# Sparse mixer: index stage reordered, with GpSimd taking part of it, and a search for the largest keys with a wait for each part

## The reference, cut to what matters

```python
def sparse_attention(h, cos, sin, w_in, q_norm, k_norm, w_out, topk):   # topk = 64, two query blocks of 128
    q, k, v, qi, ki, wi = split_cols(h @ w_in, SA_SPLITS)   # 16 heads of q, one k and v, 8 index heads qi, one ki, 8 weights wi
    q = apply_rope(rms_norm(q.reshape(b, L, ATT_HEADS, ATT_HEAD_DIM), q_norm), cos, sin)
    k = apply_rope(rms_norm(k, k_norm)[:, :, None, :], cos, sin)[:, :, 0]
    qi = apply_rope(qi...); ki = apply_rope(ki...)
    logits = einsum('bthd,bsd->btsh', qib, ki)
    score = einsum('btsh,bth->bts', relu(logits), wib) * idx_scale
    score = where(causal, score, -inf)
    _, sel = lax.top_k(score, topk)                          # the 64 keys with the largest score
    ...                                                      # softmax of q.k over the chosen keys, times v, then @ w_out
```

## Time and profile before

| what | value |
|---|---|
| median of 3 runs | 2318.72 us (2318.62 to 2319.46) |
| the profiled execution | 2319.0 us, its span 2317.1 us |
| TensorE busy | 2307.1 us (100%) |
| VectorE busy | 1682.3 us (73%) |
| ScalarE busy | 1256.1 us (54%) |
| GpSimd busy | 79.0 us (3%) |
| stretch of the sparse mixer | about 770 to 872 us from the span's start |

### The profile page before, as it was taken

One profiled execution on the slowest core, in us unless ns is written; L12 is line 12 of the kernel. 1 busy time (PEld: TensorE's weight loads), 2 busy tenths in 40 slices (PEclk: granted clock), 3 DMA queues, 4 the chain that ended last, 5 costly groups with the idle time before them and its releaser, 6 DMA issues.

```text
span 2317.1 us, 32714 instructions
## 1 busy us (share of the span) xinstructions
PE 2307.1 (100%) x13658; PEld 2019.2 (87%) x13658; DVE 1682.3 (73%) x2141; ACT 1256.1 (54%) x1523; POOL 79.0 (3%) x116
## 2 busy tenths in 40 slices
PE   9999999999999999999999999999999999999999
PEld 8889889888888978888888878888888888788887
DVE  8867846876876789768766777587687677776873
ACT  6545664554554565545555764455455467554552
POOL 2000000000000020100010000001000100000000
PEclk9999999999999999999999999999999999999999
DMA  7655435555555525655655534566556555344554
GB/s 228 195 186 178 136 138 195 186 185 186 193 191 183 169 75 189 217 188 189 197 185 181 182 128 146 167 196 210 188 189 194 183 184 169 127 149 161 197 183 145
DMA packets 335042, 409.51 MB, mean 177 GB/s; under 512 B 7894, under 2 KB 285104, under 8 KB 334896
## 3 DMA queue, kind: packets, MB, share of 16 engines
q1 hardware_dynamic: 331632, 401.66, 52.6%
q0 software_dynamic: 3072, 5.69, 0.9%
q10 hardware_dynamic: 192, 0.08, 0.0%
HBM read 406.35 MB, written 1.05 MB: 176 GB/s over the span
## 4 chain that ended last, share of the span: by engine, by line
PE 93%; DVE 4%; DMA 1%; ACT 1%; issue 0%; SPq 0%; DVEq 0%; ACTq 0%
PE bank L614 13%; PE acc L614 12%; PE bank L1384 11%; PE bank L622 7%; PE acc L622 6%; PE acc L706 6%; PE bank L706 6%; PE acc L693 4%; PE bank L713 3%; PE acc L713 3%; PE acc L790 3%; PE acc L2772 2%; PE acc L1554 2%; DVE part_lo L504 1%; PE bank L3349 1%; PE bank L652 1%
## 5 line engine op out<-in xcount | busy, mean ns | idle before, releaser
L504 DVE TENSOR_TENSOR part_lo<-raw,part_hi 128x2048 fp32r<-128x2048 f32 (+3 forms) x390 | 870.4, 2235 | 342.2 <-ACT part_hi L497 338.8
L497 ACT ACTIVATE part_hi<-raw 128x2048 fp32r<-128x2048 f32 (+3 forms) x390 | 728.3, 1868 | 331.6 <-DMA raw<-in_ffn_w 98.9
L614 PE MATMUL bank<-hT,part_hi 128*128 128x512 f32 x1408 | 328.2, 390 | 0.0
L614 PEld LDWEIGHTS bank<-hT,part_hi 128*128 128x128 f32 x1408 | 261.6, 188 | 52.9 <-ACT part_hi L497 0.2
L614 PE MATMUL acc<-hT,part_hi 128*128 128x512 f32 x1280 | 298.2, 390 | 0.0
L614 PEld LDWEIGHTS acc<-hT,part_hi 128*128 128x128 f32 x1280 | 237.7, 188 | 47.7
L1384 PE MATMUL bank<-part_hi,hT 128*128 128x512 f32 x768 | 247.4, 395 | 0.0
L622 PE MATMUL bank<-hT,part_lo 128*128 128x256 f32 x1408 | 184.2, 284 | 0.0
L622 PEld LDWEIGHTS bank<-hT,part_lo 128*128 128x128 f32 x1408 | 178.1, 192 | 3.6
L1384 PEld LDWEIGHTS bank<-part_hi,hT 128*128 128x128 f32 x768 | 144.2, 188 | 31.2 <-issue 1.7
L622 PE MATMUL acc<-hT,part_lo 128*128 128x256 f32 x1280 | 166.4, 283 | 0.2 <-DVE part_lo L504 0.2
(11 more groups left out here) (547 smaller groups left out, 3274.3 us busy)
## 6 DMA issues: line engine op xcount, KB each, us to landing
raw<-in_ffn_w SPq DMA_DIRECT2D x122, 1024.0 KB, 5.2
raw<-in_w_in SPq DMA_DIRECT2D x48, 1024.0 KB, 4.9
raw<-in_ffn_w_up SPq DMA_DIRECT2D x44, 1024.0 KB, 5.2
raw<-in_ffn_w_gate SPq DMA_DIRECT2D x43, 1024.0 KB, 5.2
raw<-in_ffn_w_down SPq DMA_DIRECT2D x32, 1024.0 KB, 5.2
raw<-in_hy_w_in SPq DMA_DIRECT2D x22, 1024.0 KB, 4.9
raw<-in_ffn_w_down SPq DMA_DIRECT2D x16, 768.0 KB, 4.4
raw<-in_ffn_w SPq DMA_DIRECT2D x12, 768.0 KB, 4.5
```

What stands on the lines that cost most here:

```text
L497: t.e.activation(part_hi[:, n % SLOTS, 0:size], raw[:, n % SLOTS, 0:size], ACT.Copy).then_inc(hi_ready, 1)
L504: t.e.tensor_tensor(part_lo[:, n % SLOTS, 0:size], raw[:, n % SLOTS, 0:size], part_hi[:, n % SLOTS, 0:size].bitcast(F32), ALU.subtract).th ...
L614: mm = pe.matmul(tiles[:, f, :].rearrange("p (h s) -> p h s", h=2), slot_cols(s, 0)[:, k, f * P:(f + 1) * P], hT[:, :, k, :], start=(first ...
```

## The change

The **index stage** gets another order. On TensorE the first token half of the fifth piece is cut in two by its contraction, with the first three index heads between; the second token half moves behind the weighted sum, and `piece_done` with it. The index heads go in groups of 3, 3 and 2 (3, 4 and 1 before). The **diagonal matrices** are made by GpSimd, in two instructions of 128x1024, released by ScalarE with `sa_weights`. **Query heads 4 to 7** are rotated by GpSimd, which also sums their squares by halving and works out the mean for all eight heads; VectorE keeps heads 0 to 3. The transposes of heads 4 to 7 wait for `sa_mid_turned`. In the **search** each part waits for its own last step. The **mask** drops the causal bias for the second part. Unused semaphores go.

```diff
@@ sparse_tensor
-            half_piece(0)
+            half_piece(0, range(0, KD // 2))
             for evicted_at in index_in:
                 pe.wait_ge(*evicted_at)
             made = index_tensor(t, range(0, 3))
-            half_piece(1).then_inc(piece_done, 1)
+            half_piece(0, range(KD // 2, KD))
...
             summed(range(0, 3))
-            made += index_tensor(t, range(3, 7))
+            t.banks.skip(1)
+            made += index_tensor(t, range(3, 6))
             summed(range(3, 5))
-            made += index_tensor(t, range(7, SA_IH))
+            t.banks.skip(1)
+            made += index_tensor(t, range(6, SA_IH))
             summed(range(5, SA_IH)).then_inc(sa_summed, 1)
+            t.banks.skip(2)
+            half_piece(1).then_inc(piece_done, 1)
...
                 if j == 1:
-                    second_flips = flip_tensor(t, lambda k, a: sa[:, a, (k + 2) * P:(k + 3) * P], 2)
+                    pe.wait_ge(sa_mid_turned, 1)
+                    second_flips = flip_banks(t, lambda k, a: sa[:, a, (k + 2) * P:(k + 3) * P], 2)
@@ sparse_scalar
             act.wait_ge(*written)
+            act.sem_inc(sa_weights, 1)
             act.activation(squares[:, 1024:1024 + TT * 64]...
-            diagonals(0)
             first = out_of(3)
             flip_scaled_scalar(t, sa_qiT, 4)
             flip_scaled_scalar(t, sa_kiT, 1)
-            diagonals(1).then_inc(sa_diag_made, 1)
             act.wait_ge(*first)
-            squares_of(tiles[3], 0)
+            squares_of(tiles[3], 0).then_inc(squares_ready, 1)
...
             index_scalar(t, range(0, 3))
             next_hi(t)
+            t.banks.skip(1)
+            index_scalar(t, range(3, 6))
+            t.banks.skip(1)
+            index_scalar(t, range(6, SA_IH))
+            t.banks.skip(2)
+            next_hi(t)
             second = out_of(4, tile_bank)
             used.clear()
             act.wait_ge(*second)
-            index_scalar(t, range(3, 7))
-            squares_of(tiles[4], 4).then_inc(squares_ready, 1)
-            index_scalar(t, range(7, SA_IH))
-            next_hi(t)
+            squares_of(tiles[4], 4).then_inc(sa_mid_squares, 1)
@@ sparse_vector
-            turn(first, 8, gained, some=slice(0, 4))
+            turn(first, 8, gained, some=early)               # early = slice(0, 4)
+            dve.wait_ge(squares_ready, t.see(squares_ready))
+            joined(first, 8, early)
+            dve.sem_inc(flip_src, 1)
+            t.link(dve.tensor_reduce(of_early(stat...), of_early(squares...), AX.X, ALU.add))
+            dve.sem_inc(norm_src, 1)
+            dve.sem_inc(sa_first_summed, 1)
             next_lo(t)
             next_lo(t)
...
-            turn(first, 8, gained, some=slice(4, 8))
-            dve.wait_ge(squares_ready, t.see(squares_ready))
-            joined(first, 8)
-            dve.sem_inc(flip_src, 2)
-            t.link(dve.tensor_reduce(stat[:, 0, 0:16], ...))
-            mean_of(0)
...
             dve.wait_ge(sa_summed, 1)
             for turn_n in range(TOPK // 8):
                 rest = acc[:, 2, :] if turn_n == 0 else sa_sc
                 for a, o, n in SA_PARTS:
-                    ins = dve.max(sa_m8[:, a, :], rest[:, o:o + n])
-                t.link(ins)
+                    if turn_n:
+                        dve.wait_ge(t.step, replaced[a])
+                    dve.max(sa_m8[:, a, :], rest[:, o:o + n]).then_inc(t.step, 1)
+                    found[a] = t.see(t.step)
                 for a, o, n in SA_PARTS:
-                    ins = dve.match_replace(sa_sc[:, o:o + n], sa_m8[:, a, :], rest[:, o:o + n], TAKEN_KEY)
-                if turn_n:
-                    t.link(ins)
-                else:
-                    t.done(ins, sa_max)
-            for a, o, n in SA_PARTS:
-                ins = dve.scalar_tensor_tensor(sa_sc[:, o:o + n], ..., sa_bias[:, o:o + n].bitcast(F32), ALU.is_gt, ALU.max)
-            t.link(ins)
-            t.link(dve.tensor_scalar(sa_sc[:, :], sa_sc[:, :], NEG, None, ALU.mult))
+                    dve.wait_ge(t.step, found[a])
+                    dve.match_replace(sa_sc[:, o:o + n], sa_m8[:, a, :], rest[:, o:o + n], TAKEN_KEY).then_inc(t.step, 1)
+                    replaced[a] = t.see(t.step)
+                if turn_n == 0:
+                    dve.wait_ge(t.step, replaced[1])
+                    dve.sem_inc(sa_max, 1)
+            # part 0: is_gt and max with the bias, as before; part 1: one tensor_scalar (is_gt, times NEG);
+            # then part 0 times NEG
@@ gpsimd
+            pool.wait_ge(sa_weights, 1)
+            for a in range(TT):
+                ins = pool.tensor_tensor(sa_diag[:, a, :, :], ident...to_broadcast([P, SA_IH, P]),
+                                         sa[:, a, SA_WI:SA_WI + SA_IH]...to_broadcast([P, SA_IH, P]), ALU.mult)
+            ins.then_inc(sa_diag_made, 1)
+            pool.wait_ge(sa_mid_squares, 1)
+            for w in (32, 16, 8, 4, 2):
+                t.link(pool.tensor_tensor(sums[:, :, :, 0:w], sums[:, :, :, 0:w], sums[:, :, :, w:2 * w], ALU.add))
+            t.link(pool.tensor_tensor(stat..., sums[:, :, :, 0:1], sums[:, :, :, 1:2], ALU.add))
+            pool.wait_ge(sa_first_summed, 1)
+            pool.tensor_scalar(stat[:, 1, 0:16], stat[:, 0, 0:16], 1.0 / SA_D, EPS, ...).then_inc(sa_mean, 1)
+            for n in range(4):
+                ins = pool.tensor_tensor(turned[n], halves_of[n % 2], sa_rope...to_broadcast([P, TT, 4, 32]), ALU.mult)
+            t.link(ins)
+            pool.tensor_tensor(halves_of[0], turned[0], turned[1], ALU.subtract)
+            t.done(pool.tensor_tensor(halves_of[1], turned[2], turned[3], ALU.add), sa_mid_turned)
```

More of the change, by code:

```diff
@@ L416, in two_blocks @@
         flip_src = sem("flip_src")
[L417 to L420, removed]
+        to_act, to_dve = sem("vector_to_scalar"), sem("scalar_to_vector")
         steps = {n: sem(f"{n}_step") for n in ("pe", "act", "dve", "pool", "sp")}
@@ L2256, in sparse_tensor, with half_piece @@
             tile_bank = claim(t, by_piece=True)
-            def half_piece(a):
-                for k in range(KD):
+            def half_piece(a, ks=range(KD)):
+                for k in ks:
                     for p, q in PASSES:
@@ L2422, in squares_of @@
                                       tile.rearrange("p a (n d) -> p a n d", d=64), ACT.Square)
[L2424 to L2428, removed]
             next_hi(t)
@@ L2548, in turn, with joined @@
                 t.link(ins)
[L2550 to L2553, removed]
+            def joined(v, heads, some=None):
+                some = some or slice(0, heads)
+                tmp = [x[:, :, some, :] for x in temps(heads)]
+                dve.tensor_tensor(v[:, :, some, 0:32], tmp[0], tmp[1], ALU.subtract)
+                t.link(dve.tensor_tensor(v[:, :, some, 32:64], tmp[2], tmp[3], ALU.add))
             plain = (cos, sin, sin, cos)
@@ L2594, in sparse_vector @@
             dve.wait_ge(taken[b], t.banks.uses[b])
-            turn(first, 8, gained, some=slice(0, 4))
+            early = slice(0, 4)
+            turn(first, 8, gained, some=early)
+            dve.wait_ge(squares_ready, t.see(squares_ready))
+            joined(first, 8, early)
+            dve.sem_inc(flip_src, 1)
+            of_early = lambda v: v[:, :, early]
+            t.link(dve.tensor_reduce(of_early(stat[:, 0, 0:16].rearrange("p (a n) -> p a n", a=TT)),
+                                     of_early(squares[:, 0:1024].rearrange("p (a n d) -> p a n d", a=TT, d=64)), AX.X, ALU.add))
+            dve.sem_inc(norm_src, 1)
+            dve.sem_inc(sa_first_summed, 1)
             next_lo(t)
@@ L2599, in sparse_vector @@
                 t.banks.take()
-            b = t.banks.take(by_piece=True)
-            dve.wait_ge(taken[b], t.banks.uses[b])
-            turn(first, 8, gained, some=slice(4, 8))
-            dve.wait_ge(squares_ready, t.see(squares_ready))
-            joined(first, 8)
-            dve.sem_inc(flip_src, 2)
[L2607 to L2613, removed]
-            mean_of(0)
-            for _ in range(4 + 4):
-                t.banks.take()
+            t.banks.take(by_piece=True)
+            for heads, passed in ((3, 1), (3, 1), (2, 2)):
+                for _ in range(heads):
+                    t.banks.take()
+                t.banks.skip(passed)
             for _ in range(2):
@@ L2625, in sparse_vector @@
             dve.wait_ge(sa_summed, 1)
+            found, replaced = [0, 0], [0, 0]
             for turn_n in range(TOPK // 8):
@@ L3869, in pieces_through @@
                 return SLOTS + sum(len(FFN_PIECES) + len(m) for m in MIXER_PIECES[:n + 1]) + n * len(FFN_PIECES)
+            pool.wait_ge(sa_weights, 1)
+            for a in range(TT):
+                ins = pool.tensor_tensor(sa_diag[:, a, :, :], ident.unsqueeze(1).to_broadcast([P, SA_IH, P]),
+                                         sa[:, a, SA_WI:SA_WI + SA_IH].unsqueeze(2).to_broadcast([P, SA_IH, P]), ALU.mult)
```

(20 more changed lines are left out.)

17 lines of the change are left out of this document (14 added, 3 removed).

## The result

The kernel before took 2319.31 us and the changed kernel 2322.72 us (medians of 20 executions each, on one chip). The ratio is 1.0013, with a 95% interval from 1.0007 to 1.0019. The change makes the kernel slower by 3.4 us, surely more than nothing and less than the 0.2% that the prediction called "no change". It had 2324.2. The profiled execution of the changed kernel took 2323.58 us, with a span of 2321.8 us, so it lies 0.9 us above the median.

What follows compares the result with a forecast made beforehand. It took TensorE, busy 2307.1 of 2317.1 us, to bound the kernel. 2319.0 + 4.8 (stall) + 2.6 (clock) - 1.9 (gain) = 2324.5, with the median 0.3 lower: 2324.2 us, range 2316.0 to 2326.5.

Steps and rivals of the forecast that it cites:

- The diagonal blocks: Index stage: GpSimd's two instructions hold VectorE's rotation, so TensorE idles 4.8 us before the index transposes; bounds 0 and 5.3.
- The clock after that wait: TensorE behind the index-stage stall: its clock falls to half, costing 2.6 us; bounds 0 and 3.4.
- What of it reaches TensorE: Softmax: earlier masks shrink TensorE's two idle stretches from 2.3 to 0.7 us; gain taken 1.9, bounds 0 and 3.1.
- The turn: Search on VectorE: one turn takes 1.22 instead of 1.44 us; eight turns save 1.8 us, bounds 0 and 2.4.
- The mask: VectorE's mask: three new instructions need 0.65 us, or up to 2.8 if each waits for GpSimd's rotations.
- First masked scores: VectorE, behind search and mask: the masks and first masked scores are ready 3.7 to 5.8 us earlier.
- heads 4 to 7: Query heads rotated on GpSimd: turned at 819.5, wanted by TensorE at 824.15; cost nothing, 4.6 us of cover.
- The argument that head 1 stands behind the seventh piece: Softmax on ScalarE: head 1's exponential follows the seventh piece's eviction, so its transposes start about 826.0 instead of 827.66.
- A: Rival: VectorE is not held by GpSimd at the index rotation, so not slower: 2316.8 us; chance 0.17.
- C: Rival: only one GpSimd diagonal instruction gets ahead of the copies, with a shorter low clock: 2320.5 us; chance 0.08.
- D: Rival: stall and clock come as forecast, but another wait holds head 0 where it was: 2326.1 us; chance 0.05.
- B: Rival: TensorE is held 4.8 us at the index transposes, but the clock stays at 2.4 GHz: 2321.6 us; chance 0.12.

Runs made afterwards that it cites:

- diag_on_scalar: The changed kernel with the diagonals back on ScalarE as 16 blocks, all else as changed: 2316.59 us.
- only_diag_on_gpsimd: The kernel before with only the diagonals made by GpSimd, released as in the changed kernel: 2323.67 us.
- late_release: The changed kernel with GpSimd's two diagonal products released by VectorE behind the copies of the index key, instead of by ScalarE: 2317.33 us.
- double_diag: The changed kernel with GpSimd making each diagonal product twice, the first time into memory that nobody reads: 2326.52 us.
- scalar_exp_first: The changed kernel with diagonals on ScalarE, and ScalarE's exponentials of head 1 put before its copy of the seventh piece: 2317.42 us.
- warm_stall: The changed kernel with 50 filler matmuls on zeros in front of TensorE's index transposes: 2320.11 us.
- small_diag: The changed kernel with GpSimd making the diagonals in eight instructions of 128x256 instead of two of 128x1024: 2320.75 us.
- only_search: The kernel before with the new search and mask alone: 2317.51 us.

## Why the prediction was right, and where it was off

**The diagonal blocks, 4.8 us of stall.** The mechanism was right and is shown: it goes with the diagonals (`diag_on_scalar`), comes with them alone (`only_diag_on_gpsimd`), goes when they are made later (`late_release`) and doubles with their number (`double_diag`).
**The clock after that wait, 2.6 us.** Right in kind: 1.2 GHz for 3.4 us, which cost 1.6. The term was taken from the 6.2 us low stretch of before, and this one is shorter.

**What of it reaches TensorE, 1.9 us.** Without stall and low clock the stretch is 76.67 us, 2.2 shorter than before. That is the gain, close to the 1.9. But TensorE doesn't idle less, as the first half of the reckoning had it (2.3 us down to 0.7). Head 0 no longer waits, head 1 waits 0.89 and head 2 0.30 us, and the waits for ScalarE and for GpSimd's rotation, 1.42 and 0.33, are new: 2.9 us in `diag_on_scalar`, 2.3 before. What became shorter is the way to the rotation, which the prediction had in its second half ("only some 1.9 us earlier"): it starts 1.8 us earlier. The other 0.4 are the clock's, near the 0.5 worked out above: at 1.2 GHz TensorE reached those transposes at 834.50, 0.5 us after the rotation's end. "With a shorter wait the clock may stay at 2.4 GHz" held in eight of eleven profiled executions with a change, but `only_diag_on_gpsimd`, whose waits aren't shorter, is one of them, and the kernel after isn't.

All together: 78.87 - 2.2 + 3.3 + 2 x 1.6 = 83.2, measured 83.18. Forecast and measured sum (5.5 and 4.3 us) are close by luck: 5.5 less 1.5 (stall), 1.0 (clock) and 0.3 (gain), plus 1.6 for a second fall of the clock that was left out. And the 4.3 are of the profiled execution; the medians differ by 3.4.

**Search, mask, heads 4 to 7.** The turn was forecast at 1.22 us and takes 1.17 to 1.19. The mask saved nothing, which its bounds allowed. First masked scores came 4.8 us earlier in `diag_on_scalar` (forecast 3.7 to 5.8); in the kernel after the stall and the low clock behind it eat that up, and they start at 35.1. GpSimd ends heads 4 to 7 at 824.74 and TensorE takes them at 829.68: 4.9 us of cover, forecast 4.6. The argument that head 1 stands behind the seventh piece was true but not the whole: `scalar_exp_first` shows two limits 0.2 us behind it, VectorE's order and the single bank, and the chain to GpSimd's rotation didn't wait for head 1: in `diag_on_scalar` its transposes end at 826.60, and ScalarE comes to its copy at 826.93.

**The rivals.** A fell with the rotation's 6.17 us, C with both products getting in ahead of the copies, D with head 0, which no longer waits (1.2 us for heads 1 and 2). B (clock stays up) fell in the profile of after; `warm_stall` brought it about, at 2320.1 us, where B had 2321.6 with its longer stall.

**Left open.** Why the clock falls behind the softmax's waits in one execution and not in another. `diag_on_scalar` and `scalar_exp_first` have nearly the same waits there (1.2 and 1.4 us) and 0 and 3.4 us of low clock, and the kernel before and `only_diag_on_gpsimd` have the same first two waits and 6.8 and 0 us. It may explain a good part of the 4.5 us over which the 20 executions of after spread (2319.83 to 2324.36); that is an inference, since only one of them has a trace. For the same reason the fall behind the stall rests on three traces with it (after, `only_diag_on_gpsimd`, `double_diag`) and on two without (`warm_stall`, `small_diag`).

## What to carry to other kernels

Work given to an idle GpSimd isn't free beside a VectorE chain on which TensorE waits without slack: each of its instructions goes in between two of VectorE's and holds the second for nearly its own length (1.70 of 1.89 us). Release such work where VectorE has slack (here 5 us later, one semaphore moved, worth 5.4 us), and price it by an instruction of the same form. When two edits each shorten the same chain, find the next limit first: here either was enough. Look for it in what other engines do behind the wait and not in the wait alone; here it was GpSimd's next rotation. The kernels `diag_on_scalar`, `late_release` and `only_search`, at 2316.6 to 2317.5 us, can't be told apart; only the first's interval lies below 1, and only just.

## What was unexpected of the hardware

Two-column instructions of VectorE took 1.66 and 1.83 us in place of 0.17, held by a product of GpSimd. A wait that runs into the time of another instruction shows as that instruction's duration, on both engines: 2.42 us for a product of 1.89. And filler of 50 matmuls on zeros in a stall kept the granted clock at 1.00 in the profiled execution, with no cost of its own (the transposes start 8.14 us behind the rotation's start, with it and without).
